# A two-layer hybrid diffusion step on one core: four edits to the order of its steps and to one broadcast

## The reference, cut to what matters

```python
h = rms_norm(x, g_pre) * (1 + scale) + shift            # adaLN, per group
(sg_u, sg_v, sg_gate, dq, dk, dv, d_gate, nq, nk, nv, n_gate, f_gate, merge) = split(h @ w_in)
y_sg   = u * (W_s norm(v) + b)                           # A
y_diff = rms_norm((softmax1 - lam * softmax2) @ v)       # B, 4 heads
y_na   = neighbourhood attention, 8 heads                # C
y_f    = real part of a 2-D DFT of h                     # D
g = sigmoid(merge)                                       # 4 x 1024
mixed = sum_b g[b] * ((y_b * silu(gate_b)) @ p_b)
out = rms_norm(mixed @ w_o, g_post)
return x + gate * out                                    # gate from the adaLN, per group
```

## Time and profile before

| | us |
|---|---|
| median of 3 runs (range) | 1982.43 (1982.02 to 1983.99) |
| the profiled execution | 1982.22 |
| its span in the profile | 1979.9 |
| PE matmul busy | 1899.4 (96%) |
| VectorE busy | 937.9 (47%) |
| ScalarE busy | 679.4 (34%) |
| GpSimd busy | 591.4 (30%) |
| mean granted clock of TensorE | 0.988 |
| chain that ended last, share of PE | 82% |

### The profile page before, as it was taken

One profiled execution on the slowest core, in us unless ns is written; L12 is line 12 of the kernel. 1 busy time (PEld: TensorE's weight loads), 2 busy tenths in 40 slices (PEclk: granted clock), 3 DMA queues, 4 the chain that ended last, 5 costly groups with the idle time before them and its releaser, 6 DMA issues.

```text
span 1979.9 us, 31247 instructions
## 1 busy us (share of the span) xinstructions
PE 1899.4 (96%) x12568; PEld 1764.7 (89%) x12568; DVE 937.9 (47%) x1505; ACT 679.4 (34%) x1295; POOL 591.4 (30%) x279
## 2 busy tenths in 40 slices
PE   7699999999999999999999999999999999999997
PEld 4697888989999999999878988988999999999996
DVE  2498788634355462421352144666254546433123
ACT  5322345524433221322352234453334332222221
POOL 2434322222222332233334332222322223323331
PEclk9899999999999999999999999999999999999999
DMA  7444421122121211122332221111212112212231
GB/s 305 149 162 148 153 96 44 54 83 67 65 65 65 96 64 54 64 75 75 128 117 75 91 75 65 48 50 44 96 65 75 54 65 95 75 35 84 75 122 59
DMA packets 51102, 172.17 MB, mean 87 GB/s; under 512 B 6800, under 2 KB 7440, under 8 KB 50960
## 3 DMA queue, kind: packets, MB, share of 16 engines
q1 hardware_dynamic: 41024, 146.60, 21.6%
q10 hardware_dynamic: 9936, 23.59, 3.4%
HBM read 162.82 MB, written 7.34 MB: 86 GB/s over the span
## 4 chain that ended last, share of the span: by engine, by line
PE 82%; DVE 10%; ACT 3%; issue 3%; DMA 1%; POOL 1%; ACTq 0%; SPq 0%; DVEq 0%; POOLq 0%
PE ps L1653 57%; PE ps L1526 4%; PE ps L1528 4%; PE ps L1527 4%; DVE mixed L1086 2%; PE ps L1760 2%; PE ps L1769 1%; PE ps L1779 1%; PE ps L1719 1%; PE ps L1734 1%; DVE nparts L1302 1%; ACT Pm L997 1%; DVE Pm L1364 1%; PE ps L1722 1%; PE ps L1804 1%
## 5 line engine op out<-in xcount | busy, mean ns | idle before, releaser
L729 POOL TENSOR_TENSOR wlo<-raw,whi 128x1024 fp32r<-128x1024 f32 x224 | 559.6, 2498 | 1238.0 <-ACT whi L786 1235.7
L1653 PE MATMUL ps<-bufA,whi 128*128 128x320 f32 x2816 | 538.4, 313 | 20.6 <-DVE vn L1204 16.3
L1653 PE MATMUL ps<-bufB,whi 128*128 128x320 f32 x2816 | 540.7, 314 | 7.1 <-DVE vn L1204 3.9
L1653 PEld LDWEIGHTS ps<-bufA,whi 128*128 128x128 f32 x2816 | 440.5, 189 | 30.4 <-issue 25.8
L1653 PEld LDWEIGHTS ps<-bufB,whi 128*128 128x128 f32 x2816 | 442.7, 190 | 16.9 <-issue 12.3
L1653 PE MATMUL ps<-bufB,wlo 128*128 128x320 f32 x1408 | 322.5, 310 | 0.0
L1653 PE MATMUL ps<-bufA,wlo 128*128 128x320 f32 x1408 | 322.0, 310 | 0.0
L786 ACT ACTIVATE whi<-raw 128x1024 fp32r<-128x1024 f32 x224 | 237.6, 1061 | 213.3 <-PE ps L1653 123.7
L1653 PEld LDWEIGHTS ps<-bufB,wlo 128*128 128x128 f32 x1408 | 236.9, 189 | 0.0
L1653 PEld LDWEIGHTS ps<-bufA,wlo 128*128 128x128 f32 x1408 | 236.3, 189 | 0.0
L1484 DVE SCALAR_TENSOR_TENSOR z<-gate_m,ps 128x640 f32<-128x640 f32 x48 | 39.4, 822 | 226.3 <-PE ps L1653 225.9
(11 more groups left out here) (226 smaller groups left out, 2035.5 us busy)
## 6 DMA issues: line engine op xcount, KB each, us to landing
raw<-in_wstream SPq DMA_DIRECT2D x224, 512.0 KB, 3.3
stage<-in_wstream SPq DMA_DIRECT2D x32, 512.0 KB, 4.3
stage<-in_w_mod SPq DMA_DIRECT2D x16, 512.0 KB, 12.6
out_y_sample<-X ACTq DMA_DIRECT2D x8, 512.0 KB, 2.6
Pm<-in_rpb ACTq DMA_DIRECT2D x12, 256.0 KB, 3.3
X<-in_x_sample SPq DMA_DIRECT2D x4, 512.0 KB, 5.4
xres<-in_x_sample ACTq DMA_DIRECT2D x4, 512.0 KB, 5.7
xres<-out_y_sample ACTq DMA_DIRECT2D x4, 512.0 KB, 5.3
```

The costliest lines, as they stand in the source:

```text
L729: pool.tensor_tensor(wlo[:, s % SPLITS, :], raw[:, s % RAWS, :], whi[:, s % SPLITS, :].bitcast(F32), ALU.subtract).then_inc(sems["lo"], 1)
L1653: ins = pe.matmul(ps[:, 2 * b + n, 0:HALF], wt[:, cols], src[:, part, base + k, n * HALF:(n + 1) * HALF], start=k == 0 and wt is hi and pa ...
```

## The change

1. **Opening.** LSG stands before TK 6 and loads gvb first. LAM moves behind the first F step (sgg 0) of layer 0. The floor of chunk 5, and so of 6 and 7, is VN 4: ScalarE and GpSimd split them after the squares and powers of VS.
2. **Attention.** `differential()` takes the pieces itself: one ahead of S 0, then two after each S (one in units 0, 5 and 10) and one after each EX, one before TP 19 and one before PV 19, four after the last NR. The gate multiplication of d_gate leaves its F step and becomes a step FG, put after the two pieces behind S or after CB. YT f-1 stands after the S of the first unit of head f+1 (after CB 19 for YT 2).
3. **Gate broadcast.** One DG (one VectorE operation over 128x512, from a tiled 32x32 identity `eye`) and one GR: four matmuls, each of 32 rows of the contraction by 512 columns, into banks 4 to 7; ScalarE copies them in two operations. GR uses neither projection buffer. The order of branch 2 becomes M0 DG M1 P0 GR P1 FD0 M2 M3 P2 P3 FD1 M4 M5 P4 P5 FD2 M6 M7 P6 P7 FD3, then FA.
4. **Edge.** The statistics, H and Xb of the tiles before stand between the quarters of wo1; H 3 stands ahead of sgv, Xa 4 and Xb 4 within it. A chunk that was to be split at the fourth quarter of sgv's tile 0 is split at VN 4.

```diff
-def differential():
+def differential(pieces):
...
+    some(1, out)
     for u, (f, hh, t) in enumerate(units):
-        out += [("S", "diff", u, f, hh, t, 0)] + norm + [None]
-        norm = []
+        out.append(("S", "diff", u, f, hh, t, 0))
+        flush(norm)
+        some(1 if u in (0, 5, 10) else 2, late)
+        flush(late)
...
-        out += [("EX", "diff", u, f, hh, t), None]
+        out.append(("EX", "diff", u, f, hh, t))
+        some(1, late)
...
-        if f and t == 3:
-            late = [("YT", "diff", f - 1)]
+        if f and t == 4:
+            norm = [("YT", "diff", f - 1)]
...
-    for c in range(2):
-        last.insert(1 + 8 * c, ("DG", c))
-        last.insert(6 + 8 * c, ("GR", c))
     for g in range(GROUPS):
-        last.insert(4 + 4 * g, ("FD", g))
+        last.insert(4 + 5 * g, ("FD", g))
+    last.insert(1, ("DG",))
+    last.insert(4, ("GR",))
     last.append(("FA",))
...
-            add(l, *V((0, 0), (0, 1), (1, 0), (1, 1)), ("H", 3), ("HL", 3), *V((0, 2), (1, 2), (2, 0), (2, 1), (2, 2)), ("H", 4), ("HL", 4), ("LSG",),
-                *V((0, 3), (1, 3), (2, 3), (0, 4), (1, 4), (2, 4)))
+            add(l, *V((0, 0), (0, 1)), ("Xa", 4), *V((1, 0), (1, 1)), ("Xb", 4), ("HL", 3), *V((0, 2), (1, 2), (2, 0), (2, 1)), ("H", 4),
+                *V((2, 2),), ("LSG",), *V((0, 3), (1, 3)), ("HL", 4), *V((2, 3), (0, 4), (1, 4), (2, 4)))
...
-            add(l, *[("T", "wo1", p, j) for p in range(4)])
-            add(l, ("Ya", j))
+            part = [("T", "wo1", p, j) for p in range(4)]
+            add(l, *part[:2])
             if j:
                 add(l + 1, ("Xa", j - 1))
             if j >= 2:
                 add(l + 1, ("H", j - 2))
-            add(l, ("Yb", j))
+            add(l, part[2])
             if j:
                 add(l + 1, ("Xb", j - 1))
+            add(l, part[3], ("Ya", j))
             if j >= 2:
                 add(l + 1, ("HL", j - 2))
+            add(l, ("Yb", j))
             add(l + 1, ("XS", j))
-        add(l + 1, ("Xa", TILES - 1), ("Xb", TILES - 1))
+        add(l + 1, ("H", 3))
...
-        lead_in = [("HK", 0), ("HK", 2), ("HK", 4), ("HK", 6), ("HL", 7)]
+        lead_in = [("HK", 0), ("HK", 2), ("HK", 4), ("HK", 6), ("HL", 7), ("VN", TILES - 1)]
...
+            if self.layer[self.first_of_slot[n]] and i == self.at[1, ("T", "sgv", 3, 0)]:
+                i = self.at[1, ("VN", TILES - 1)]
...
+                        for name in ("expd", "atready", "pvfree", "kout"):
+                            pe.wait_ge(sems[name], count.before(name))
+                        for r in range(4):
+                            rows_of = slice(32 * r, 32 * r + 32)
+                            ins = pe.matmul(ps[:, 4 + r, :], ones[rows_of, :], diag[rows_of].rearrange("p k c j -> p (k c j)"),
+                                            start=True, stop=True)
+                        ins.then_inc(sems["gready"], 1)
```

More of the change, by code:

```diff
@@ L255, in layer_middle @@
     for f in range(4):
-        s += [("F", "sgg", f)] + some(1) + [("F", "sgu", f)] + some(1) + [("SG", f)] + some(f < 3)
+        s += [("F", "sgg", f)] + [("LAM",)] * (l + f == 0) + some(1) + [("F", "sgu", f)] + some(1) + [("SG", f)] + some(f < 3)
     s += [("FENCE",), ("LAT",)]
@@ L265, in layer_middle @@
     s += [("FENCE",), ("VO", "dv")]
-    rest = interleave(differential(), parts([("F", "dgate", f) for f in range(4)] + branch(0)))
+    rest = differential(parts([("F", "dgate", f) for f in range(4)] + branch(0)))
     before = min(rest.index(("P", 0, 2)), rest.index(("YT", "diff", 0)))
@@ L310, in plan @@
     for k in range(2, KT):
[L311 removed]
+        add(0, ("HK", k), ("HL", k), *[("LSG",)] * (k == KT - 1), ("TK", k - 1))
         if k % 2 == 0 and k < 6:
@@ L315, in plan @@
             add(0, ("WK", k // 2 + 1))
-    add(0, ("LSG",), ("LAM",), ("TK", KT - 1))
+    add(0, ("TK", KT - 1))
     V = lambda *pj: [("T", "sgv", p, j) for p, j in pj]
@@ L865, in _ @@
                             act_e.wait_ge(sems["store"], count.before("store"))
+                        load(gvb[:], A["sg_norm_g"][layer].partition_broadcast(P))
                         load(wsT[:], A["sg_wT"][layer])
                         load(bsb[:], A["sg_b"][layer])
-                        load(gvb[:], A["sg_norm_g"][layer].partition_broadcast(P))
                     elif kind == "LAT":
@@ L1041, in _ @@
                     elif kind == "GR":
[L1042 to L1044 removed]
+                        act_e.wait_ge(sems["gready"], count.step("gready"))
+                        for c in range(2):
+                            act_e.activation(grow[:, c, :].rearrange("p (k r j) -> p r k j", r=4, j=32),
+                                             ps[:, 4:8, :].rearrange("p r (k c j) -> p r k c j", c=2, j=32)[:, :, :, c, :],
+                                             ACT.Copy).then_inc(sems["gcopied"], 1)
+                            act_e.wait_ge(sems["gcopied"], count.own("gcopied"))
                     elif kind == "LEND":
@@ L1270, in _ @@
                             dve.wait_ge(sems[f"free{b}"], count.own(f"free{b}"))
+                    elif kind == "FG":
+                        f = step[1]
+                        dve.wait_ge(sems["tanhd"], count.step("tanhd", ("F", "dgate", f)))
+                        dve.scalar_tensor_tensor(halves(G[:, f, :]), halves(G[:, f, :]), 1.0, dsplit(b),
+                                                 ALU.add, ALU.mult).then_inc(sems[f"free{b}"], 1)
+                        dve.wait_ge(sems[f"free{b}"], count.own(f"free{b}"))
                     elif kind == "VT":
@@ L1838, in _ @@
                     elif kind == "GR":
-                        pe.wait_ge(sems["diag"], count.step("diag", ("DG", step[1])))
-                        for k in range(KT):
-                            ins = pe.matmul(dflat(b, 1024)[:, k * P:(k + 1) * P], ones[:], diag[:, k, :], start=True,
-                                            stop=True)
-                        ins.then_inc(sems["dready"], 1)
+                        pe.wait_ge(sems["diag"], count.step("diag", ("DG",)))
+                        for name in ("expd", "atready", "pvfree", "kout"):
[5 more added lines that the diff above has]
+                        ins.then_inc(sems["gready"], 1)
                 for name, n in count.phase(PLAN.last):
```

70 lines of the change are left out of this document (42 added, 28 removed).

## The result

The changed kernel takes 1989.85 us (median of 6 runs, 1989.49 to 1991.68); the kernel before, on the same chip, 1982.68 us (6 runs, 1979.80 to 1983.99). The ratio is 1.004, 95% interval [1.003, 1.0051]: 8 us slower, where 8 us faster was forecast, and 4 us above the range. The profiled run is one of 1989.49 us, with a span of 1986.8 against 1979.9.

A forecast was written before the change was run, and what follows sets the result against it. TensorE was taken to bound the kernel. From 1982.2 us, opening -8, attention -11, broadcast -5.1, P 3's stall -2.7, FD 3 +22.6 and edge -4.4 summed to -8.6, giving 1974 us, range 1959 to 1986.

The forecast's parts named there:

- opening: Start of layer 0: shorter VN wait, partly lost to a new stop at sgg 1; -8 us, from -5 to -14.
- attention: Differential attention, both layers: half of PE's waits go through moved pieces, FG and YT; -11 us, from -4 to -17.
- gate broadcast with P 3's stall: Branch 2, both layers: four row quarters run together, -5.1 us; PE's wait for P 3's eviction goes, -2.7.
- FD 3 ahead of FA: End of branch 2, both layers: PE waits 8.4 us for FD 3, then halved clock; +22.6 us, from +16 to +24.
- edge: Between the layers: VN wait goes, -6.8, Xb wait changes, +2.4; together -4.4 us, from -12 to +4.
- what YT brings in: Attention: M step after YT waits for the tanh, 0.85 us twice a layer; at YT 3, 1 to 2 us left.
- The VN wait with its clock: Edge: the 3.9 us wait on VN and its clock drop go, as the chunk moves behind the statistics; -6.8 us.
- The new order: Edge: H enters the statistics chain; 5.9 us of waiting and a clock drop for 3.9 and a drop; +2.4 us.
- the chain per tile: Edge: time from one tile's squares to the next grows from 6.4 to 8.8 us, making H 2 1.3 us late.
- rival A: Edge's chain goes on: PE also waits at HL 3 and Xb 4, +10 instead of -4.4; 1997 or 1987; chance 0.14.

The follow-up runs named there:

- x4: Kernel before with only the opening's part (LSG earlier with gvb first, LAM behind sgg 0, chunks 5 to 7 split behind VN 4): 1971.99 us, ratio 0.9947.
- x5: Kernel before with only the attention's part (counted pieces in the differential attention, gate product as step FG): 1981.01 us, ratio 0.9994.
- x6: Kernel before with only the gate broadcast (DG, GR and eye), FD at its old places: 1973.38 us, ratio 0.9957.
- x1: Changed kernel with the four FD steps at places 4, 8, 12, 16 of branch 2 instead of 4, 9, 14, 19: 1970.07 us, ratio 0.9937.
- x2: Changed kernel with the whole edge between the layers as before, including the place of the chunk split: 1987.43 us, ratio 1.0028.
- x10: x1 with gvb's load counted on its own semaphore, LAM ahead of sgg 0, chunks 5 and 6 at sgg 0: 1971.07 us, ratio 0.9944.
- x14: x1 with gvb's load counted on its own semaphore, LAM and DM 0 behind sgu 0: 1971.79 us, ratio 0.9949.
- x7: x1 with YT f-1 issued after CB of head f's fourth unit, two pieces between the last head's NR 1 and NR 2: 1968.49 us, ratio 0.9928.
- x3: Changed kernel with the edge's order as before, but quarter 3's chunk still split at VN 4: 1982.1 us, ratio 0.9992.
- x13: x1 with x3's edge (order as before, only quarter 3's chunk behind the statistics): 1959.47 us, ratio 0.9882.
- x8: x1 with the chunks of sgv's quarters 1 and 2 split after Xb 3, in the new edge order: 1968.77 us, ratio 0.9931.
- x11: x13 with the chunk of sgv's quarter 1 split at Ya 4 and quarter 2's at Xa 4: 1960.26 us, ratio 0.9891.

## Why the prediction was wrong

| part | predicted | measured, by ratios to before |
|---|---|---|
| opening | -8 | -10.5 (x4; -7.1 by the spans) |
| attention | -11 | -1.2 (x5) |
| gate broadcast with P 3's stall | -7.8 | -8.5 (x6) |
| FD 3 ahead of FA | +22.6 | +20.4 (after against x1) |
| edge | -4.4 | +2.4 (after against x2) |
| sum | -8.6 | +2.6, where the whole measured +7.9 |

Each measured part has an interval of 3 to 4 us to either side, so that 5 us between their sum and the whole are no more than their uncertainty; that the parts hinder each other by a few microseconds isn't excluded, and stays open.

- **The opening** was right in mechanism and nearly in size. One step of it was wrong without harm: "gvb is issued some 10 us earlier, and sgg 0 can start at about 63.7" overlooked that VN waits for all three loads of LSG. It started at 66.3, and the stop at sgg 1 was 4.2 us for 7. That these two make up for one another is what x10 showed: VectorE's queue, where DM 0 stands ahead of sgu 0's eviction, sets sgg 1's start; x14 moved the stop to the next buffers.
- **FD 3** was right in place, releaser and blocked first operation: 8.4 us said, 8.3 measured in both layers, and a halved clock behind it. This term alone decided the sign of the result, and it was in the sum.
- **The gate broadcast** was right: 1.0 us said, 1.07 measured, so the four row quarters run together. By the Trainium skill's page TensorEngine Tiling (Theoretical Speedup), up to four times for 32 rows; 3.56 us in turn to 1.07 is 3.3 times, so the trace agrees with the bound. The same page of the Trainium skill (Key Properties) says that a change of tiling mode drains the engine. Ahead of the next matmul the trace leaves at most 0.18 us for that, by which 1.07 is over a quarter of 3.56.
- **The attention** is the first failed step, 10 us. It was "waits now 9.6 to 12.5 us a layer with the tail, and 4 of clock; I keep half of the waits". The waits of 0.9, 1.51 and 1.73 us did go. The prediction priced what YT brings in at "0.85 us now, twice a layer" (the trace of before has 0.4 and 0.9), and YT 3 at 1 to 2. The trace of after has 0.94, 2.10, 0.71 and 2.22 a layer, and 1.26 on AT that the prediction didn't name. The rows at 352 to 357 us show how the 2.10 comes about: YT's product on VectorE (L1446) now stands behind the next S's reduces, ScalarE's rounding of it behind the product, and the tanh of the M step (gate_m) behind the rounding. x7, with YT elsewhere, has 0.3 us on gate_m. The idle time stayed at 12.7 and 9.8 us. To keep half of a gain for new waits, without pricing each from rows, was a guess with the look of an estimate. The rest is the clock (named at 4 us a line before, but left out of the 11, which is half of 9.6 plus 12.5): x5's profile shows 0.97 in layer 1 where the one before shows 0.99.
- **The edge** is the second, 7 us, and within it one term. The VN wait with its clock was -6.8 and measured -7.1. The new order was "+2.4" and measured +9.5 (x3) and +10.9 (x13). Even on the prediction's own terms the number doesn't add up: 5.9 us of waiting for 3.9, with a drop in both, is +2.0, and the H work that comes into the chain is 1.51 and 1.06 us with a gap between them, up to 3.9 us from its first row to its last in the earlier trace rows, not 2.4. Two steps of it then failed. The larger is the chain per tile, said to be 8.8 us and measured at 9.4, so that H 2 is 2.8 us late and not 1.3. The smaller is H 3, said to be 4.6 us late and measured at 9.0, as the chunks of sgv's quarters 1 and 2 come to stand ahead of Xa 3's power in GpSimd's queue. The prediction had moved only the one chunk that the diff names. That other chunks' issue points are given by step indices, so that a reordering of the steps moves them against the statistics, was not looked at. x8 tells the two apart: without these chunks the order leaves PE waiting 0.4, 2.8 and 3.9 us before H 1 to H 3, against the 3.4 of the old one, and is still 9.7 us slower than x13 by the ratios. Of the 7.4 in the windows, 4.8 are idle time, where the prediction said 2.0, and 2.7 busy time at the lower clock, where it said nothing. The chunks themselves are worth 1.2 us by the ratios, within the noise.

So rival A, the edge's chain going on, came closest in kind and number (1987 to 1997), though through other instructions than it named: it had GpSimd's splits hold VectorE, and the waits were on the chain of statistics and on GpSimd's own queue; HL 3 and Xb 4 were in time. Its 1987 is no sum of its terms: with two of the three they give 0.4, 8.8 or 11.8 us, not 5. The rest of its sum, a weak attention, was right. Its chance of 0.14 was too low for a mechanism whose place was known and whose two parts were both only bounded from one side.

## What to carry to other kernels

A wait that goes by name may only move to another step of the same in-order queues: x5, x7, x10, x11 and x14 each removed waits of 2 to 7 us by name, others came in their place, and the time stayed within the intervals. Compare the idle sum of the stage, not the wait.
A step at the very end of a branch, ahead of the first consumer of its result, has no cover left; moving FD 1, 2 and 3 by one, two and three places put the last against FA, and that cost 20.4 us.
In a plan where transfers and conversions are issued at step indices, list after every reordering what each queue now has ahead of the latency chain: here two conversions of 2.4 us came to stand before a power of 0.55 and made a wait of 3.9 us into one of 9.0. And add the chain up from its rows: x8 shows that most of what this reordering lost was the chain of each tile, 9.4 us for 6.4.

## What the runs showed of the hardware that was not expected

- A VectorE operation on a handful of numbers can last as long as GpSimd's split beside it: 2.33 us for 5 numbers in a partition in x7, against 0.17 for the same operation of other heads in x7, and L1191 takes 4.42 us in the changed kernel and 2.29 without a split beside it. Not every operation is held: L1293, one of whose two inputs lies in PSUM, takes 0.82 us in the changed kernel also where it starts within a split (at 114.88 and 131.03 us). The Trainium skill's page SBUF — State Buffer (Terms) says of the pair of ports that VectorE and GpSimd share that the loser "fully blocks"; the trace agrees for these two, and the price is up to nearly a whole split, however small the operation.
- The granted clock doesn't fall behind each wait of the same length. The changed kernel has the wait of 2.10 us on gate_m in both layers. In layer 0 the matmuls behind it start at 1.2 GHz (1.41 us for four, the row is above), in layer 1 they stay at 2.4 GHz; the row of layer 1, and a window behind each wait:

```profile
1330.11 0.82 PE L1688 MATMUL ps<-bufB,whi 128*128 128x320 f32 x4 [2.10 <-ACT gate_m L1061]
```
```profile
358.00:360.00 2.00, 2.00 (x9) 2.00 (x9) 0.00 (x0) 0.00 (x0) 2.00 (x1) 0.50 0.00 0
...
1332.00:1334.00 2.00, 2.00 (x16) 2.00 (x14) 0.00 (x0) 1.64 (x5) 1.60 (x1) 1.00 0.00 0
```

So one drop comes and goes between profiles of the same code (2.4 us of PE's busy time in the attention of before against x6), and a stage's entry in the table is good to no more than that.
